# Two feature pairs instead of one go by halves of the tokens at the four norm joints of a three-block float32 kernel

## The chip, the cores and the metric

The kernel runs on one core of one Trainium2 chip. The metric is the device time of one execution in microseconds (us); a lower number is better. The engines are named as in the profile: PE is TensorE (its weight loads are PEld), DVE is VectorE, ACT is ScalarE, POOL is GpSimd and SP is SyncE, which here only issues transfers.

## The reference, cut to what matters

512 tokens of width 1024 go through a first block (mixer, then a mixture of 32 experts) and a second block of two layers:

```
x = first_block(x, ...)            # mixer, hier_moe (32 experts, 2 per token), rmsnorm(x, norm_final)
h = layer_norm(x, ln_in_g, ln_in_b)
for l in range(2):
    proj = h @ w_in[l]             # q, k, v, u
    a = diff_attention(q, k, v)    # 8 heads, softmax(s1) - lam * softmax(s2)
    f = fourier_mix(u, w_f[l], b_f[l])
    h = layer_norm(ALPHA * h + concat(a, f) @ w_o[l], ln1_g[l], ln1_b[l])
    g, up = split(h @ w_gu[l])     # 2 x 2816 columns
    h = layer_norm(ALPHA * h + (silu(g) * up) @ w_down[l], ln2_g[l], ln2_b[l])
return h
```

So a product follows each norm, and the product can only begin for those tokens whose norm is done.

## The kernel before, in words

**Products.** Every product of the second block is done in float32 accuracy by three matmuls (`mm3`, lines 507 to 509): weights and data are each split into a high part (fp32r) and the rest, and hi\*hi, hi\*lo and lo\*hi are added in PSUM. Weights come in chunks of 128 x 1024 values. SP loads a chunk into one of four raw cells (line 464); ACT copies it to its high part (`hi_to`, line 483); DVE subtracts to get the low part (`lo_to`, line 493). The parts lie in a ring of three slots; a chunk named in the list `apart` of `halves_places` takes a fourth slot, and then the ring goes on without it. A chunk may be converted when the product that used its slot last has counted `w_used`. A product of one feature pair (2 x 128 output features, 512 tokens) uses two chunks and 48 matmuls (`gemm_feat`).

**A norm joint.** There are four: the experts' sum with the final and the first norm (`*_final`), the norm behind `w_o` of each layer (`*_wo`), and the one behind `w_down` of layer 0 (`*_ffn`). The 512 tokens are four tiles. For each tile DVE adds the residual and takes statistics, POOL the root, ACT applies the norm (line 690; 2284 at the first joint), PE transposes it (line 599, `turn_pe`), ACT scales it (622) and writes the high part (626), and DVE writes the rest (630, 636). PE does the last chunks of the product ahead tile by tile between the transposes (`gemm_tail`), and then `feat_halves`: the first feature pair behind the norm, at first for tokens 0 to 255 (24 matmuls of 256 columns for one feature tile, the last tile's transposes, 24 more), and, when the last tile is done, for tokens 256 to 511 (48 more). The second feature pair follows as a whole by `gemm_feat` with 48 matmuls of 512 columns. In the feed-forward part the pairs are named gate and up, in the mixer Q and K.

**The barrier.** `meet` drains PE, ACT, DVE and POOL and lets each go on when all four have come. It stands at the end of `*_wo` and `*_ffn`, on PE behind `feat_halves`. The first joint has none.

**The mixer's start.** ACT issues five small loads (2601 to 2605), copies Q (2610), converts two chunks, splits the 128 x 128 constants and `w_f` (2613, 2615), loads the table of Exp and copies K (2620); DVE makes the low parts (2688 to 2715). PE forms an outer product of the two split constants (`w_mm`, 6 matmuls, waits for `spl` from DVE line 2708) and then the scores (2529), which wait for K's low part.

**Between experts and the second block.** The last experts' rows are scattered to DRAM (`s_y`) by POOL (2146). When the scatters have landed, four reloads are issued by SP (2259) and four by ACT (2274), two for each token tile. The vectors of the final and first norm are loaded by ACT (2102 to 2104), each broadcast to 128 partitions (512 KB).

**The down projection.** `gemm_tok` does 11 chunks for each half of the output. Its first matmul waits until POOL has written the low part of the last activation (2986).

## Time and profile before

| | |
|---|---|
| median of 3 runs | 2004.35 us (2002.73 to 2006.64) |
| the profiled execution: time, span | 2006.64 us, 2005.4 us |
| PE busy | 1838.4 us, 92% of the span |
| DVE, ACT, POOL busy | 958.5, 777.3, 394.9 us |
| mean granted clock of TensorE | 0.967 |

The time is that of a whole execution; the span is that between the first and the last instruction in its profile. PE is busy for 92% of the span, so the question at each place is for what PE waits there. Timeline rows give start, duration, engine, line, operation, output and input, a count, and in brackets the idle time before and what ended it. ACTq and SPq rows are transfers being issued.

### The profile page before, as it was taken

How to read it: one execution, taken by the hardware profiler on the slowest of the kernel's cores; microseconds unless marked ns; L12 is line 12 of the kernel's file. 1: busy time of each engine (PE TensorE's matmuls, PEld its weight loads, DVE VectorE, ACT ScalarE, POOL GpSimd, SP SyncE). 2: the span in 40 equal slices, each digit the busy share in tenths (PEclk: the TensorE clock that was granted, in tenths of full speed). 3: DMA queues.
4: the chain of work that ended last, by engine and by line, in shares of the span. 5: the costliest groups of instructions: out<-in, count | busy, mean ns of one | idle time of the engine just before them, and what ended most of it. 6: DMA issues, size and time to landing. Idle time of an engine off the chain costs nothing.

```text
span 2005.4 us, 26563 instructions
## 1 busy us (share of the span) xinstructions
PE 1838.4 (92%) x10396; PEld 1449.7 (72%) x10396; DVE 958.5 (48%) x1881; ACT 777.3 (39%) x1436; POOL 394.9 (20%) x438
## 2 busy tenths in 40 slices
PE   7999999996998754998999999999999999999997
PEld 6888777785544424776778888787876778888786
DVE  4458776663311015968454433234868454333234
ACT  3344476221433234665253233115566252332212
POOL 1019155102222111243011111000233012111001
PEclk9999999996999996998999999999998999999999
DMA  4244200576999983211323333232211233333231
GB/s 162 80 113 126 95 2 2 168 286 242 381 383 401 394 308 125 74 53 43 105 85 100 100 95 95 89 100 70 77 64 43 84 95 98 101 95 95 87 103 53
DMA packets 134884, 264.43 MB, mean 132 GB/s; under 512 B 11616, under 2 KB 92128, under 8 KB 122464
## 3 DMA queue, kind: packets, MB, share of 16 engines
q1 hardware_dynamic: 116320, 228.35, 33.1%
q10 hardware_dynamic: 13312, 25.90, 3.8%
q0 software_dynamic: 5120, 8.40, 1.3%
q8 instruction: 85, 1.39, 0.3%
q14 instruction: 47, 0.39, 0.1%
HBM read 254.22 MB, written 16.78 MB: 135 GB/s over the span
## 4 chain that ended last, share of the span: by engine, by line
PE 54%; DMA 9%; DVE 7%; ACT 3%; issue 2%; POOL 1%; PEld 1%; PEldq 0%; ACTq 0%; POOLq 0%; SPq 0%; DVEq 0%
PE b L507 15%; PE b L508 15%; PE b L509 15%; DMA m<-in_w_gate_up 6%; PE b L2023 3%; ACT m L622 2%; DVE m L2736 1%; DMA m<-in_w_down 1%; PE b L2561 1%; PE b L2048 1%; PE b L2543 1%; PE b L2529 1%; DMA s_h<-m 1%; ACT m L690 1%; DVE m L694 1%
## 5 line engine op out<-in xcount | busy, mean ns | idle before, releaser
L507 PE MATMUL b<-m,m 128*128 128x512 f32 (+3 forms) x2060 | 782.0, 380 | 28.4 <-DVE m L636 8.8
L508 PE MATMUL b<-m,m 128*128 128x512 f32 (+3 forms) x2060 | 772.6, 375 | 0.0
L509 PE MATMUL b<-m,m 128*128 128x512 f32 (+3 forms) x2060 | 772.5, 375 | 0.0
L493 DVE TENSOR_TENSOR m<-m,m 128x1024 fp32r<-128x1024 f32 (+1 forms) x212 | 278.2, 1319 | 497.5 <-ACT m L483 496.6
L507 PEld LDWEIGHTS b<-m,m 128*128 128x128 f32 x2060 | 392.6, 191 | 105.8 <-issue 22.1
L509 PEld LDWEIGHTS b<-m,m 128*128 128x128 f32 x2060 | 392.4, 190 | 67.5
L508 PEld LDWEIGHTS b<-m,m 128*128 128x128 f32 x2060 | 393.1, 191 | 64.1
L483 ACT ACTIVATE m<-m 128x1024 fp32r<-128x1024 f32 (+1 forms) x236 | 245.7, 1048 | 484.2 <-PE b L509 458.0
L2986 POOL TENSOR_TENSOR m<-m,m 128x512 fp32r<-128x512 f32 x44 | 71.1, 1636 | 422.1 <-ACT m L2932 422.1
L2023 PE MATMUL b<-m,m 128*64 128x256 f32 x1024 | 126.7, 390 | 27.5 <-DMA m<-in_w_gate_up 26.2
L2023 PEld LDWEIGHTS b<-m,m 128*64 128x64 f32 x1024 | 73.6, 139 | 78.9 <-issue 38.6
L2111 DVE SCALAR_TENSOR_TENSOR m<-m,m,b 64x256 f32<-64x256 f32 x32 | 15.4, 482 | 215.6 <-ACT m L2090 215.6
L2636 ACT ACTIVATE m<-m,m 128x512 f32<-128x512 f32 x128 | 91.0, 712 | 57.5 <-DVE m L2736 57.5
L2776 POOL TENSOR_TENSOR m<-m,m 128x1024 fp32r<-128x1024 f32 x24 | 61.8, 2573 | 175.5 <-PE b L2529 175.5
L2736 DVE CUSTOM_DVE_ANT_0 m<-b,m 128x512 f32<-128x512 f32 x128 | 80.6, 685 | 18.2 <-PE b L2529 18.2
L682 POOL TENSOR_TENSOR m<-m,m 128x1 f32<-128x1 f32 x20 | 13.7, 685 | 362.4 <-DVE m L678 330.6
L599 PE MATMUL b<-m,m 128*128 128x128 f32 x160 | 26.0, 315 | 52.5 <-ACT m L2284 33.0
L2048 PE MATMUL b<-m,m 128*64 128x512 f32 x256 | 62.0, 603 | 8.8 <-DMA m<-in_w_down 7.3
L2932 ACT ACTIVATE m<-m 128x512 fp32r<-128x512 f32 x44 | 27.8, 632 | 97.1 <-DVE m L2952 96.0
L599 PEld LDWEIGHTS b<-m,m 128*128 128x128 f32 x160 | 20.9, 161 | 59.2 <-ACT m L2284 34.7
L2099 ACT ACTIVATE m<-b 64x512 f32<-64x512 f32 x64 | 37.9, 592 | 51.0 <-PE b L2048 50.2
L2952 DVE TENSOR_TENSOR m<-b,m 128x512 f32<-128x512 f32 x44 | 30.2, 692 | 52.4 <-PE b L509 52.4
(339 smaller groups left out, 1896.2 us busy)
## 6 DMA issues: line engine op xcount, KB each, us to landing
m<-in_w_gate_up SPq DMA_DIRECT2D x64, 1024.0 KB
m<-in_w_gu SPq DMA_DIRECT2D x88, 512.0 KB, 3.5
m<-in_w_down SPq DMA_DIRECT2D x32, 1024.0 KB
m<-in_w_in SPq DMA_DIRECT2D x48, 512.0 KB, 3.8
m<-in_w_down SPq DMA_DIRECT2D x44, 512.0 KB, 3.7
m<-in_w_in SPq DMA_DIRECT2D x20, 448.0 KB, 3.6
m<-in_w_o SPq DMA_DIRECT2D x16, 512.0 KB, 3.8
s_gt<-m ACTq DMA_DIRECT2D x16, 256.0 KB, 2.1
```

Of the source, the lines that this page charges most:

```text
L483: e.activation(flat(whi[HX[i]], i), flat(raw[cell], i), ACT.Copy).then_inc(sem("w_hi"), 1)
L493: e.tensor_tensor(flat(wlo[HX[i]], i), flat(raw[RX[i][0]], i), fr(flat(whi[HX[i]], i)), ALU.subtract).then_inc(sem("w_lo"), 1)
L507: e.matmul(out, xh, yh, start=start, stop=False, skip_group_check=True)
L508: e.matmul(out, xh, yl, start=False, stop=False, skip_group_check=True)
L509: return e.matmul(out, xl, yh, start=False, stop=stop, skip_group_check=True)
L599: m = e.transpose(bank[b][:, k * P:k * P + P], src[:, (4 * g + k) * P:(4 * g + k + 1) * P], ident)
L2023: m = e.matmul(bank[i][CAP * h:CAP * h + CAP, 0:256], XT[i][:, k, :], w[:, kk, 256 * h:256 * h + 256], start=k == 0, stop=k == 7, skip_gro ...
L2048: m = e.matmul(bank[2 + i][CAP * h:CAP * h + CAP, :], AT[i][:, f, :], w[:, 0, 512 * h:512 * h + 512], start=f == 0, stop=f == 1, skip_grou ...
L2636: e.activation(x, x, ACT.Exp, bias=sm2[:, 0, 4 * s + j:4 * s + j + 1], scale=-1.0, accum_out=sm2[:, 2, 4 * s + j:4 * s + j + 1]).then_inc( ...
L2736: e.tensor_tensor_reduce(EE[s % 2][j], bank[j][:, :], m, 2.0 ** -(h + 1), 3e38, ALU.add, ALU.min, sm2[:, 0, w:w + 1]).then_inc(sem("m_m"), 1)
L2776: e.tensor_tensor(flat(wlo[HX[i]], i), flat(raw[RX[i][0]], i), fr(flat(whi[HX[i]], i)), ALU.subtract).then_inc(sem("w_lo"), 1)
L2986: e.tensor_tensor(FAl[:, k, :], UP[f], fr(FAh[:, k, :]), ALU.subtract).then_inc(sem("ff_l"), 1)
```

## The change

**The joints.** `feat_halves` now takes two feature pairs (four chunks, four banks). The first token half is done for both pairs, then the second half for both. The last tile's transposes come after the first feature tile at the first joint, and after the second one at the three others. The whole `gemm_feat` of the second pair (K, or the first up) is gone, so that `meet` now stands behind both pairs. The third and fourth chunk are converted ahead of ACT's and DVE's work on the third tile's gain (`t == 3`), no longer at the joint's end. `mix0` joins the chunks that have the fourth slot. Layer 1 swaps banks 0 to 3 with 4 to 7, in the mixer's outer product and scores too.

**The first joint.** The norm vectors are loaded by SP ahead of the first mixer chunks (`sync_gains`), and all eight reloads of `s_y` are issued by SP. The conversions of the first four mixer chunks stand at the start of `*_final`. ACT applies the norm of the last tile behind the gain of the third.

**The down projection.** Its first matmul waits for the bank and the first two activations only; after each chunk it waits for the next two (`after_down`).

```diff
-        HX, HB = halves_places(len(chunks), (CH["gu0"], CH["mix1"], CH["gu1"]), WHOLE)
+        HX, HB = halves_places(len(chunks), (CH["mix0"], CH["gu0"], CH["mix1"], CH["gu1"]), WHOLE)
...
-        def feat_halves(e, name, c0, xhi, xlo, bs, u, amid):
+        def feat_halves(e, names, c0, xhi, xlo, bs, u, amid, free):
-            w = [chunk(e, c0), chunk(e, c0 + 1)]
+            w = []
             for half in range(2):
                 c = slice(256 * half, 256 * half + 256)
                 e.wait_ge(*at("tr_lo", 8 * u + 4 * half + 4))
+                for q in range(2):
+                    if half == 0 and q == 1:
+                        free(e)
+                    for f, k in [(f, k) for f in range(2) for k in range(8)] if half == 0 else [(f, k) for k in range(8) for f in range(2)]:
+                        if half == 0 and f == 0 and k % 4 == 0:
+                            w.append(chunk(e, c0 + 2 * q + k // 4))
+                        hi, lo = w[2 * q + k // 4]
+                        sl = slice(f * P, f * P + P)
+                        m = mm3(e, bank[bs[2 * q + f]][:, c], hi[:, k % 4, sl], lo[:, k % 4, sl], xhi[:, k, c], xlo[:, k, c], k == 0, k == 7)
+                        if half == 1 and k == 7 and f == 0:
+                            m.then_inc(sem("mm_" + names[q]), 1)
+                        if half == 0 and k == 7:
+                            amid(2 * q + f)
+                    if half == 1:
+                        m.then_inc(sem("w_used"), 2)
...
         def vector_layer_norm(e, n, before, hi, lo, chunk_to):
                 ln_stats(e, n, t)
+                if t == 3:
+                    lo_to(e, chunk_to + 2)
...
         def scalar_layer_norm(e, n, hi, banks, chunk_to):
             for t in range(NT):
+                if t == 3:
+                    hi_to(e, chunk_to + 2)
...
-            return (lambda t: one(t - 1) if t > 0 else None), (lambda f: one(3) if f == 0 else None)
+            return (lambda t: one(t - 1) if t > 0 else None), (lambda n: one(3) if n == 1 else None)
...
+        def sync_gains(e):
+            last = max(i for i, cells, _ in LOADS if cells[0] in (TAIL + 4, GAINS))
+            e.wait_ge(*at("w_used", last + 2))
+            e.dma_start(gF, io["norm_final"].partition_broadcast(P)).then_inc(sem("gF"), 16)
+            e.dma_start(gL, io["ln_in_g_2"].partition_broadcast(P)).then_inc(sem("gL"), 16)
+            e.dma_start(bL, io["ln_in_b_2"].partition_broadcast(P)).then_inc(sem("gL"), 16)
...
             for t in range(NT):
+                e.dma_start(YA[2 * t], Y2[t * P:t * P + P, :]).then_inc(sem(f"ya{2 * t}"), 16)
                 e.dma_start(YA[2 * t + 1], Y2[S + t * P:S + t * P + P, :]).then_inc(sem(f"ya{2 * t + 1}"), 16)
...
         def scalar_final(e):
-            added_up(e)
-            for t in range(NT):
-                e.dma_start(YA[2 * t], Y2[t * P:t * P + P, :]).then_inc(sem(f"ya{2 * t}"), 16)
             e.dma_start(LNT, io["c_lnT"]).then_inc(sem("lnT"), 16)
+            hi_to(e, CH["mix0"] + 4)
...
         def tensor_mixer(e, l):
             c0 = CH[f"mix{l}"]
-            gemm_feat(e, f"k{l}", c0 + 2, NHhi, NHlo, 8, (6, 7), no_wait)
...
-            feat_halves(e, f"fg{l}", CH[f"gu{l}"], NHhi, NHlo, (0, 1), 3 + 2 * l, amid)
+            feat_halves(e, (f"fg{l}", f"up{l}"), CH[f"gu{l}"], NHhi, NHlo, swapped(l, (0, 1, 2, 3)), 3 + 2 * l, amid, lambda e: e.wait_ge(*at(f"res_wo{l}", 8)))
             meet(e)
...
             def free_down(e, j, t):
-                if t == 0:
-                    e.wait_ge(*at("ff_l", 22 * l + 22))
+                if t == 0 and j == 0:
+                    e.wait_ge(*at("ff_u", 22 * l + 20))
+                    e.wait_ge(*at("ff_l", 22 * l + 2))
+
+            def after_down(e, u):
+                if u < 10:
+                    e.wait_ge(*at("ff_l", 22 * l + 2 * u + 4))
...
         def sync_program(e):
             sync_norm1(e)
-            load_chunks(e, 0, CH["mix0"] + RAW)
+            load_chunks(e, 0, CH["mix0"])
+            sync_gains(e)
+            load_chunks(e, CH["mix0"], CH["mix0"] + RAW)
             sync_final(e)
```

**What the instructions look like in order.** On ACT, at layer 0's first norm joint, before: the gain of the last tile (m_56 and m_57, to m_214), the third and fourth chunk's high parts (into ring slots m_59, m_60 from raw cell m_54), and behind the barrier (`s_meet`) the feed-forward part.

```order
L622 ACTIVATE m_56<-b,m_206 128x128 [waits s_tr_lo,s_tr_pe]
L622 ACTIVATE m_56<-b,m_206 128x128 x3
L622 ACTIVATE m_57<-b,m_206 128x128 [waits s_tr_pe]
L622 ACTIVATE m_57<-b,m_206 128x128 x3
L626 ACTIVATE m_214<-m_56 128x4x128 [waits s_at_p]
L483 ACTIVATE m_59<-m_54 128x1024 [waits s_w_used,s_w_raw0]
L483 ACTIVATE m_60<-m_54 128x1024 [waits s_w_used,s_w_raw1]
L2913 DMA m_263<-in_ln_g 128x1024 [waits s_meet]
L2914 DMA m_264<-in_ln_b 128x1024
L2928 ACT_TABLE_LOAD
L2928 ACTIVATE m_259<-b 128x512 [waits s_mm]
```

The same place of the change, from the norm of the third tile to the gain of that tile, and then the rows about the barrier:

```order
L696 ACTIVATE m_127<-m_127,m_205 128x1024 [waits s_ln_nm]
L483 ACTIVATE m_58<-m_54 128x1024 [waits s_w_used,s_w_raw0]
L483 ACTIVATE m_59<-m_54 128x1024 [waits s_w_used,s_w_raw1]
L628 ACTIVATE m_56<-b,m_206 128x128 [waits s_tr_lo,s_tr_pe]
L628 ACTIVATE m_56<-b,m_206 128x128 x3
L628 ACTIVATE m_57<-b,m_206 128x128 [waits s_tr_pe]
L628 ACTIVATE m_57<-b,m_206 128x128 x3
L632 ACTIVATE m_214<-m_56 128x4x128 [waits s_at_p]
```

```order
L628 ACTIVATE m_57<-b,m_206 128x128 x3
L632 ACTIVATE m_214<-m_56 128x4x128 [waits s_at_p]
L2937 DMA m_263<-in_ln_g 128x1024 [waits s_meet]
L2938 DMA m_264<-in_ln_b 128x1024
L2952 ACT_TABLE_LOAD
L2952 ACTIVATE m_259<-b 128x512 [waits s_mm]
L2952 ACTIVATE m_260<-b 128x512 [waits s_w_used]
L483 ACTIVATE m_60<-m_55 128x1024 [waits s_w_used,s_w_raw2]
L483 ACTIVATE m_58<-m_55 128x1024 [waits s_w_used,s_w_raw3]
```

The two conversions (L483) moved from just ahead of the barrier to ahead of the third tile's gain; the rows behind the barrier are the same, but the fifth and sixth chunk (m_60 and m_58) are now the first that PE needs there, where before they were the third and fourth.

On SP, at the end of the experts' weights (m_136, m_137), before: the first mixer chunks (m_54, m_55) and the four reloads.

```order
L468 DMA m_136<-in_w_down 128x2048
L468 DMA m_137<-in_w_down 128x2048
L464 DMA m_54<-in_w_in 128x4x256 x2
L464 DMA m_55<-in_w_in 128x4x256 x2
L2259 DMA m_217<-s_y 128x1024
L2259 DMA m_219<-s_y 128x1024
L2259 DMA m_221<-s_y 128x1024
L2259 DMA m_223<-s_y 128x1024
```

And in the change:

```order
L468 DMA m_137<-in_w_down 128x2048
L2263 DMA m_201<-in_norm_final 128x1024
L2264 DMA m_202<-in_ln_in_g 128x1024
L2265 DMA m_203<-in_ln_in_b 128x1024
L464 DMA m_54<-in_w_in 128x4x256 x2
L464 DMA m_55<-in_w_in 128x4x256 x2
L2271 DMA m_216<-s_y 128x1024
L2272 DMA m_217<-s_y 128x1024
L2271 DMA m_218<-s_y 128x1024
L2272 DMA m_219<-s_y 128x1024
L2271 DMA m_220<-s_y 128x1024
L2272 DMA m_221<-s_y 128x1024
```

The three norm vectors (m_201 to m_203) now lie between the experts' weights and the mixer's chunks, and the reloads have become eight in a row, of which six are shown.

On ACT, at the start of the first mixer, before: the fourth chunk (m_59), five small loads, the copies of Q (to m_225), and the fifth and sixth chunk.

```order
L483 ACTIVATE m_59<-m_55 128x1024 [waits s_w_used,s_w_raw3]
L2601 DMA m_249<-in_c_c 128x256
L2602 DMA m_250<-in_w_f 128x4x128
L2603 DMA m_211<-in_lam_params 128x128
L2604 DMA m_212<-in_subln_g 128x1
L2605 DMA m_213<-in_b_f 128x4
L2610 ACTIVATE m_225<-b,m_209 128x512 [waits s_mm,s_bo]
L2610 ACTIVATE m_225<-b,m_209 128x512 [waits s_w_used]
L483 ACTIVATE m_60<-m_54 128x1024 [waits s_w_used,s_w_raw0]
L483 ACTIVATE m_58<-m_54 128x1024 [waits s_w_used,s_w_raw1]
L2613 ACTIVATE m_251<-m_249 128x256 [waits s_w1v]
```

And in the change:

```order
L2621 DMA m_249<-in_c_c 128x256
L2622 DMA m_250<-in_w_f 128x4x128
L2623 DMA m_211<-in_lam_params 128x128
L2624 DMA m_212<-in_subln_g 128x1
L2625 DMA m_213<-in_b_f 128x4
L2630 ACTIVATE m_225<-b,m_209 128x512 [waits s_mm,s_bo]
L2630 ACTIVATE m_225<-b,m_209 128x512 [waits s_w_used]
L483 ACTIVATE m_59<-m_54 128x1024 [waits s_w_used,s_w_raw0]
L483 ACTIVATE m_60<-m_54 128x1024 [waits s_w_used,s_w_raw1]
L2633 ACTIVATE m_251<-m_249 128x256 [waits s_w1v]
L2635 ACTIVATE m_253<-m_250 128x512 [waits s_g1]
```

The fourth chunk's conversion is gone from here. The sixth chunk now goes to m_60, the slot of the third chunk, which both versions free only when PE has used it; in the change that is at the end of K.

## Rows read from the trace of the kernel before

**Rows 1.** The page's first part, PE; then the waits of PE in total.

```profile
PE 1838.4 (92%) x10396; PEld 1449.7 (72%) x10396; DVE 958.5 (48%) x1881; ACT 777.3 (39%) x1436; POOL 394.9 (20%) x438
...
PE b L599 <- ACT m L2284: 33.0, 3, 25.9
...
PE b L507 <- DVE m L636: 8.8, 5, 2.8
...
PE b L507 <- POOL m L2986: 6.9, 2, 3.4
```

**Rows 2.** Timeline, experts' end to second block: start us, us, what, idle before it.

```profile
738.94 0.89 POOL L2146 DMA_INDIRECT s_y<-m,m  x1 [7.13 <-ACT m L2099]
...
742.48 0.89 POOL L2146 DMA_INDIRECT s_y<-m,m  x1 [2.65 <-ACT m L2099]
...
742.89 0.49 ACTq L2104 DMA_DIRECT2D m<-in_ln_in_b  x1
...
751.01 2.01 SPq L2259 DMA_DIRECT2D m<-s_y  x4
...
756.08 1.23 DVE L2307 TENSOR_TENSOR m<-m,m 128x1024 f32<-128x1024 f32 x1 [9.90 <-DMA m<-s_y]
...
782.20 0.55 PE L507 MATMUL b<-m,m 128*128 128x256 f32 x1 [2.85 <-DVE m L636]
```

**Rows 3.** DMA queues: windows 740:741, 747:748; then L2104's own landing.

```profile
q0 software_dynamic: 27, 0.11, 50.0%
...
q0 software_dynamic: 47, 0.10, 26.3%
...
DMA to landing us min/median/max: 8.3/8.3/8.3
```

**Rows 4.** Timeline of PE at layer 0's first norm joint.

```profile
1020.59 1.09 PE L599 MATMUL b<-m,m 128*128 128x128 f32 x8 [1.54 <-ACT m L690]
...
1026.02 0.38 PE L507 MATMUL b<-m,m 128*128 128x256 f32 x1 [1.48 <-DVE m L636]
...
1031.76 0.28 PE L509 MATMUL b<-m,m 128*128 128x256 f32 x1
1032.29 0.47 PE L507 MATMUL b<-m,m 128*128 128x512 f32 x1 [0.26 <-PEq L439]
...
1043.03 0.39 PE L509 MATMUL b<-m,m 128*128 128x512 f32 x1
```

**Rows 5.** Timelines of ACT and DVE behind that joint.

```profile
1032.12 0.34 ACTq L2913 DMA_DIRECT2D m<-in_ln_g  x1
...
1035.23 1.06 ACT L483 ACTIVATE m<-m 128x1024 fp32r<-128x1024 f32 x1
...
1036.39 1.23 DVE L493 TENSOR_TENSOR m<-m,m 128x1024 fp32r<-128x1024 f32 x1 [8.16 <-ACT m L483]
```

**Rows 6.** Timelines of ACT, DVE and PE at layer 1's mixer.

```profile
1406.59 0.34 ACTq L2601 DMA_DIRECT2D m<-in_c_c  x1
...
1412.58 1.06 ACT L483 ACTIVATE m<-m 128x1024 fp32r<-128x1024 f32 x1 [1.38 <-PE b L509]
...
1410.70 0.23 DVE L2688 TENSOR_TENSOR m<-m 128x64 f32<-128x64 f32 x1 [8.00 <-DMA m<-in_lam_params]
...
1415.15 0.69 DVE L2708 TENSOR_TENSOR m<-m,m 128x512 fp32r<-128x512 f32 x1
...
1419.33 0.51 PE L2529 MATMUL b<-m 32*128 32x512 f32 x4
```

**Rows 7.** Timeline of PE: layer 0's first scores.

```profile
810.88 0.51 PE L2529 MATMUL b<-m 32*128 32x512 f32 x4
```

**Rows 8.** PE at layer 0's down projection; then windows, PEclk behind POOL.

```profile
1264.44 0.77 PE L507 MATMUL b<-m,m 128*128 128x512 f32 x1 [3.43 <-POOL m L2986]
...
1264.40:1267.40 3.00, 2.96 (x7) 2.41 (x8) 0.98 (x1) 0.00 (x0) 0.00 (x0) 0.50 0.18 46
1267.40:1272.00 4.60, 4.60 (x21) 3.73 (x21) 0.00 (x0) 0.27 (x1) 0.00 (x0) 0.98 0.22 84
```

More of the change, by code:

```diff
@@ L581, in feat_halves @@
                 e.wait_ge(*at("tr_lo", 8 * u + 4 * half + 4))
-                for f, k in [(f, k) for f in range(2) for k in range(8)] if half == 0 else [(f, k) for k in range(8) for f in range(2)]:
-                    hi, lo = w[k // 4]
-                    sl = slice(f * P, f * P + P)
-                    m = mm3(e, bank[bs[f]][:, c], hi[:, k % 4, sl], lo[:, k % 4, sl], xhi[:, k, c], xlo[:, k, c], k == 0, k == 7)
-                    if half == 1 and k == 7 and f == 0:
-                        m.then_inc(sem("mm_" + name), 1)
-                    if half == 0 and k == 7:
-                        amid(f)
-            m.then_inc(sem("w_used"), 2)
+                for q in range(2):
[13 more added lines that the diff above has]
+                        m.then_inc(sem("w_used"), 2)
         def turn_pe(e, u, t, src, banks):
@@ L2342, in gpsimd_second, with lb, swapped @@
             c.inc(e.iota(TOE.bitcast(I32), pattern=[[-1, 896]], base=384, channel_multiplier=1))
+        def lb(l):
+            return bank[4 * l:] + bank[:4 * l]
+        def swapped(l, banks):
+            return tuple(b ^ (4 * l) for b in banks)
         NST = 16
@@ L2400, in block_job @@
             c0 = CH[f"mix{l}"] + BLK[f"{kind}{n - n % 2}"]
-            o = bank[jbank[j]]
+            o = lb(l)[jbank[j]]
             for tt in range(2 if kind == "V" else 1):
@@ L2420, in tensor_job @@
             kind, n = j[0], int(j[1])
-            o = bank[jbank[j]]
+            o = lb(l)[jbank[j]]
             bank_free(e, l, j, s)
@@ L2457, in scalar_job @@
             kind, n = j[0], int(j[1])
-            o = bank[jbank[j]]
+            o = lb(l)[jbank[j]]
             if kind not in "VQKUCD":
@@ L2481, in vector_job @@
             kind, n = j[0], int(j[1])
-            o = bank[jbank[j]]
+            o = lb(l)[jbank[j]]
             if kind in "UV":
@@ L2528, in tensor_scores @@
                     r = slice(32 * j, 32 * j + 32)
-                    m = e.matmul(bank[j][:, :], QT[a][r, p, qt * P:qt * P + P], KT[b][r, p, :], start=i == 0, stop=i == 2, skip_group_check=True)
+                    m = e.matmul(lb(l)[j][:, :], QT[a][r, p, qt * P:qt * P + P], KT[b][r, p, :], start=i == 0, stop=i == 2, skip_group_check=True)
                     if i == 2:
@@ L2548, in tensor_values @@
             p, half = m_ // 2, m_ % 2
-            o = bank[6][:, 256 * half:256 * half + 256]
+            o = lb(l)[6][:, 256 * half:256 * half + 256]
             e.wait_ge(*at("m_h", NST * l + 2 * m_ + 2))
@@ L2609, in scalar_mixer @@
                 q0_done(e, l, x)
-                e.activation(QT[0][:, x, :], bank[4 + x][:, :], ACT.Copy, scale=qsc[:, x:x + 1]).then_inc(sem("qk0_h"), 1)
+                e.activation(QT[0][:, x, :], lb(l)[4 + x][:, :], ACT.Copy, scale=qsc[:, x:x + 1]).then_inc(sem("qk0_h"), 1)
             hi_to(e, c0 + 3 + HL)
@@ L2658, in scalar_turn_p @@
             turned_free(e, l, k)
-            e.activation(*turned(k, 0), ACT.Copy).then_inc(sem("m_h"), 1)
+            e.activation(*turned(l, k, 0), ACT.Copy).then_inc(sem("m_h"), 1)
         def scalar_out(e, l, p):
@@ L2665, in scalar_out @@
                 e.wait_ge(*at("n_l", 4 * l + p - 1))
-            e.activation(OO[p % 2], bank[6][:, :], ACT.Copy).then_inc(sem("m_o"), 1)
+            e.activation(OO[p % 2], lb(l)[6][:, :], ACT.Copy).then_inc(sem("m_o"), 1)
             if p > 0:
                 job_done(e, l, f"B{p - 1}")
-            e.activation(SQ, bank[6][:, :], ACT.Square).then_inc(sem("m_o"), 1)
+            e.activation(SQ, lb(l)[6][:, :], ACT.Square).then_inc(sem("m_o"), 1)
         def scalar_normed(e, l, p):
```

82 lines of the change are left out of this document (38 added, 44 removed).

## Prediction

> **What bounds the kernel now.** I read the page first, then PE's waits in total, then the timeline at each place that the diff touches. PE is busy for 92% of the span, and each single reason for which it waits is small [rows 1]. The largest here is the first joint (33.0 us before the transposes). The change aims at it only at its edges. The others that it touches are the wait for the last tile's low part (8.8 us in 5 waits) and the start of the down projection (6.9 us in 2 waits). PE alone sets the pace behind the experts. So for each place I ask when PE's next matmul can start, and whether ACT and DVE have its operands ready by then.
>
> **The change part by part.**
>
> *1. Between experts and first joint.* POOL issues the last scatter of expert rows from 742.48 to 743.37, and ACT issues the norm vectors up to 743.4; SP gets the scatters' landing at 751.01, and the first pair of reloads is there at 756.08 [rows 2]. The last norm vector landed 8.3 us after its issue at 742.89, at 751.2 [rows 3]: at the same moment as the scatter. The scatter before was issued at 738.94 to 739.83 [rows 2] and its packets ran at 740 to 741, while those of the last one mostly wait until 747 [rows 3]. I read this as the scatter standing among 1.5 MB of norm vectors. In the change these are issued behind the last expert weights and ahead of the mixer's chunks. If the last scatter then needs what the one ahead of it did (through by about 742.5, so 2.7 us from the end of its issue), SP starts at 743.4 + 2.7 = 746.1 instead of 751.0: 4.9 us. The first pair's second reload is now issued 0.5 us behind the first on one queue (four issues take 2.01 us). Term: -4.5 us, with bounds of -5.4 (scatter through in 1.8 us) and 0 (it was late for another reason). The first four conversions on ACT and DVE are done by about 750 and lie in this wait.
>
> Here the Trainium skill ("DMA: Bandwidth & Descriptors", Queues, rings and completion order) speaks against this term: each DMA engine goes round between the queues that have work, a packet at a time. By that rule a scatter beside the vectors' queue would have been through soon, and their removal would bring little. The rows of queue 0 do not bear it out here (its packets come at 747), but they do not show the cause either.
>
> *2. Layer 0's norm joint, up to the barrier.* Before: the first feature tile ends at 1020.59 - 1.54 = 1019.05, PE waits 1.54 us for the last tile's norm, transposes, does the second feature tile, waits 1.48 us, and does the second half [rows 4]. From 1026.02 to 1031.76 lie 47 matmuls of 256 columns: 0.12 us each, 5.8 us for 48; from 1032.29 to 1043.03 lie 47 of 512: 0.228 us each, 10.97 us for 48. So a pair in halves costs 0.6 us more than whole. The pair "up" now ends at about 1043.3. After: from 1019.05 PE goes on with the second feature tile (2.9 us, to 1021.9), transposes (1.0 us), first half of the second pair (5.8), both second halves (11.6): the end is 1040.2. Does anything stop it? ACT has two conversions (1.06 us each [rows 5]) ahead of the third tile's gain, and waits for the product ahead to end, so the last tile's norm, which PE had at 1020.59, comes at about 1021.8: just in time. The last tile's low part follows its transposes by some 4.5 us (1026.02 - 1021.68 [rows 4]), and 5.8 us of second pair cover it. So both waits go, and PE stands at the barrier 3.1 us earlier than it finished the same work before.
>
> *3. Behind that barrier.* Before, PE had the whole pair "up" (11 us) there, and its chunks had been made ready ahead of `meet`. In that cover ACT issued two loads, loaded a table, did both Silu, and converted the next chunk from 1035.23; DVE's low part came from 1036.39 to 1037.62 [rows 5]. That is 5.5 us after ACT's first issue at 1032.12. Now PE's next product (gate of i = 1) needs this very chunk; nothing converts it earlier, since `chunk_to + 2` ends with the fourth. So PE stands still from 1040.2 for 0.25 us of barrier and 5.5 us of ACT and DVE, until about 1046.0: 2.7 us later than before (1043.3).
>
> *4. The clock.* After 3.43 us of idle time PE restarts at 1264.44 with a granted clock of 0.50, the 1.2 GHz level, until about 1267.4, and is at 0.98 on average behind it [rows 8]. Half of 3 us is a loss of 1.5 us. The waits of 1.5 us [rows 4] show nothing like it. Each new stall is longer than 3.4 us, so I add 1.5 us to each. Items 2 to 4 give +4.3 us for this joint and, with the same code in layer 1, +8.6 us for both.
>
> *5. Layer 1's mixer.* The joint is the same and lies 374.5 us later (ACT's first issue behind it is at 1406.59, not 1032.12 [rows 5, 6]), so its two pairs end at 1414.6. Only then ACT starts its five loads. In the trace ACT begins them at 1406.59, DVE is held until 1410.70 by the load of the lambdas, and is then busy nearly without a gap until `w_f` is split at 1415.15 + 0.69 = 1415.84 [rows 6]: 9.25 us. ACT's wait for PE in it (1.38 us) isn't on this chain. PE's outer product waits for it: 1414.6 + 0.25 + 9.25 = 1424.1. At half pace 6 matmuls take 2.6 us, and K's low part is there by then, so the scores start at 1426.7 to 1427.0 instead of 1419.33 [rows 6]. Term: +7.5 us (+6.3 if the clock stays up).
>
> *6. Layer 0's mixer.* No barrier here: the small loads and Q's copies stay hidden. The first half starts at 782.20 [rows 2] (all shifted by item 1). Counted back from the scores at 810.88 [rows 7]: outer product 1.6, whole K 11.0, second half 5.8, a wait like that of item 2 (1.6) leave the second feature tile's end at 790.9; with the second pair's first half (5.8) and both second halves (11.6) behind it, less the 0.3 between them that goes, the end is 808.0. The sixth chunk's slot becomes free only then, and on ACT its conversion stands ahead of the constants, `w_f`, and K. From such a conversion at 1412.58 to the split `w_f` at 1415.84 layer 1 took 3.3 us [rows 6], so the outer product starts at 808.0 + 0.25 + 3.3 = 811.5, and with a halved clock the scores start at 814.2 instead of 810.88. Term: +3.4 us (+2.5 at full clock).
>
> *7. Down projections.* The wait of 3.43 us [rows 8] goes in both layers: the first two activations and the bank are long ready, and the last activation is needed only after 10 chunks of 5.5 us. With the 1.5 us at half clock behind it: -5.0 us each, -10.0 us.
>
> Sum: -4.5 + 8.6 + 7.5 + 3.4 - 10.0 = +5.0 us, on the profiled execution's 2006.64 us. That one lies 2.3 us above the median, so I predict 2004.35 + 5.0, about 2009.5 us. The banks and the swap cost nothing: the products' count and sizes stay, and no bank is waited for by this reading.
>
> **The rivals.**
>
> *A, faster:* the stalls behind the barriers and in front of the outer products don't come, because the next chunk's conversion turns out to lie ahead of the barrier. Then each joint gives its 2.7 us (1043.3 - 1040.2, less 0.4 of barrier), the first mixer about 1 us, and the sum is -4.5 - 8.1 - 1 - 10.0 = -24 us: 1980 us. Against it: the order on ACT has that conversion behind the rows with `s_meet`. It decides as soon as the restart takes less than 2.7 us instead of 5.5. Chance 0.07.
>
> *B, the scatter isn't held by the norm vectors:* the DMA engines serve both in turn, and the scatter is late through something of its own. Then SP starts at 751.0 as before and item 1 is 0: 2009.5 + 4.5 = 2014 us. For it: its first packets do run beside the vectors; against it: the scatter ahead of it was quick [rows 3]. Chance 0.2. It is the case that the Trainium skill's rule in item 1 stands for.
>
> *C, the clock doesn't fall* in the new stalls, or only for a part: 4 x 1.5 less, 2003.5 us, no change to be measured. For it: only one restart is read here. Against it: it is the only kind of restart from more than 3 us that this place shows [rows 8]. Chance 0.13.
>
> *D, the down projection's wait comes back* as one for a weight chunk (the third chunk's slot is freed only when the last "up" ends): 2009.5 + 10 = 2019.5 us. Against it: two chunks are ready, 11 us of work, and ACT and DVE need 2.3 us for a chunk. Chance 0.05.
>
> **How the numbers follow.** My forecast (all seven items) has 0.55. The range must reach to B and to C: 2002 to 2016 us. Two executions of this kernel differ by up to 3.9 us, so 0.2% (4 us) is about what can be told from no change. Slower (over 2008.4): most of the forecast, B and D; same: C and the forecast's lower edge; faster: A and little else. That gives 0.60 slower, 0.30 same, 0.10 faster.
>
> **What would show it.** In the profile after: no wait of PE for DVE's last low part (line 636's counterpart) behind the second layer norms; new waits of PE for the low part of a weight chunk (493) of 5 to 6 us behind both `*_wo`, about 9 us for the split of `w_f` in layer 1 and 3 to 4 us in layer 0; granted clock 0.50 after each; no wait for the activation's low part at the down projections; SP's reloads about 3 us after the last scatter's issue, not 8. I am wrong if PE passes the barriers without a stall, or if the scatter still lands 7.6 us after its issue.

## The result, and the profile after

The change takes 2009.66 us (median of 12 runs, 2006.6 to 2014.37), the kernel before beside it 2004.47 us (12 runs, 2000.53 to 2008.14). The ratio is 1.0022 (95% interval 1.0014 to 1.0031), so the change is slower by 5.2 us, and the forecast said 5.0. The profiled execution took 2009.88 us with a span of 2008.3 us and a mean granted clock of 0.961, where before had 0.967.

The page's first part of the change, PE; then PE's waits in total. They answer to [rows 1].

```profile
PE 1840.8 (92%) x10588; PEld 1463.3 (73%) x10588; DVE 956.6 (48%) x1881; ACT 776.5 (39%) x1436; POOL 395.0 (20%) x438
...
PE b L605 <- ACT m L2294: 30.5, 3, 23.4
...
PE b L507 <- DVE m L493: 16.3, 5, 5.7
PE b L507 <- DVE m L2728: 12.7, 2, 9.3
...
PE b L507 <- DVE m L642: 2.7, 1, 2.7
```

The reader is to see that PE's busy share has not moved while its list of waits has. The wait for POOL's last activation at the down projection (6.9 us) is gone, and of the 8.8 us for the last tile's low part 2.7 are left, all at the first joint. Two waits have grown in their place: one for the low part of a weight chunk (L493) and one for the low part of `w_f` (L2728), which is not among the waits of before. For the weight chunks before had this row:

```profile
PE b L507 <- DVE m L493: 4.9, 3, 2.0
```

The timeline of the change between experts and first joint, as in [rows 2]:

```profile
740.48 0.89 POOL L2151 DMA_INDIRECT s_y<-m,m  x1 [2.65 <-ACT m L2109]
745.34 0.34 ACTq L2285 DMA_DIRECT2D m<-in_c_lnT  x1
745.73 3.90 ACT L483 ACTIVATE m<-m 128x1024 fp32r<-128x1024 f32 x4 [6.02 <-issue]
746.58 0.34 SPq L2271 DMA_DIRECT2D m<-s_y  x1
746.81 4.63 DVE L493 TENSOR_TENSOR m<-m,m 128x1024 fp32r<-128x1024 f32 x4 [13.30 <-ACT m L483]
...
751.55 1.23 DVE L2323 TENSOR_TENSOR m<-m,m 128x1024 f32<-128x1024 f32 x1
```

SP starts the reloads 5.2 us after the end of the last scatter's issue (741.37), where before it was 7.6 us. ACT passes the branch at the experts' end in 6 us without work and converts the first four chunks only behind it. DVE's four low parts end at 751.4, just when the first sum begins.

The timeline of PE at layer 0's norm joint, as in [rows 4], then those of ACT and DVE behind the barrier, as in [rows 5]:

```profile
1018.77 1.04 PE L605 MATMUL b<-m,m 128*128 128x128 f32 x8
...
1036.56 0.28 PE L507 MATMUL b<-m,m 128*128 128x256 f32 x1
...
1042.80 0.77 PE L507 MATMUL b<-m,m 128*128 128x512 f32 x1 [5.73 <-DVE m L493]
```

```profile
1037.16 0.33 ACTq L2937 DMA_DIRECT2D m<-in_ln_g  x1
...
1040.27 2.00 ACT L483 ACTIVATE m<-m 128x1024 fp32r<-128x1024 f32 x2
...
1041.43 2.36 DVE L493 TENSOR_TENSOR m<-m,m 128x1024 fp32r<-128x1024 f32 x2 [17.33 <-ACT m L483]
```

The last tile's transposes stand without idle time, and PE then runs at 0.12 us for each matmul of 256 columns up to the barrier. There it stops for 5.73 us, until ACT and DVE have loaded a table, done the two Silu and converted the fifth chunk.

The timelines of PE at the two mixers' starts, as in [rows 6, 7]:

```profile
803.88 0.28 PE L509 MATMUL b<-m,m 128*128 128x256 f32 x1
807.56 0.80 PE L507 MATMUL b<-m,m 128*128 128x512 f32 x1 [3.40 <-DVE m L2728]
...
810.41 0.80 PE L2550 MATMUL b<-m 32*128 32x512 f32 x4
...
1410.21 0.28 PE L509 MATMUL b<-m,m 128*128 128x256 f32 x1
1419.74 0.77 PE L507 MATMUL b<-m,m 128*128 128x512 f32 x1 [9.25 <-DVE m L2728]
...
1422.57 0.80 PE L2550 MATMUL b<-m 32*128 32x512 f32 x4
```

Busy time in windows of the change, the granted clock behind POOL's column: behind layer 0's barrier, over the start of layer 0's down projection, and at layer 0's mixer, as in [rows 8]:

```profile
1042.80:1045.90 3.10, 3.10 (x7) 2.48 (x8) 3.10 (x4) 1.47 (x3) 0.70 (x1) 0.50 0.61 184
...
1249.00:1280.00 31.00, 31.00 (x139) 25.66 (x138) 8.64 (x8) 8.60 (x10) 2.54 (x2) 1.00 0.32 102
...
807.50:810.40 2.90, 2.84 (x6) 1.82 (x6) 2.13 (x6) 1.72 (x4) 0.00 (x0) 0.50 0.58 181
810.40:813.80 3.40, 3.40 (x21) 2.64 (x21) 2.44 (x7) 1.45 (x4) 0.00 (x0) 0.50 0.00 0
```

The clock falls to its 1.2 GHz level behind each new stall. The down projection begins without a stall and at full clock.

**Where the 5 us are.** I cut both profiles at the same seven starts on PE and at the end of the last scatter's issue (743.37 before, 741.37 after). That leaves out everything ahead, where the code is the same and single profiles differ by some us. Each column is one execution.

| stretch (us) | before | after | difference | predicted |
|---|---|---|---|---|
| last scatter to first halves | 38.83 | 36.20 | -2.6 | -4.5 (item 1) |
| to layer 0's first scores | 28.68 | 32.84 | +4.2 | +3.4 (item 6) |
| to layer 0's last scores | 129.06 | 127.31 | -1.8 | 0 |
| to the first transposes behind `w_o` | 63.39 | 62.61 | -0.8 | 0 |
| to those behind `w_down` (joint, down) | 374.45 | 373.41 | -1.0 | -0.7 (items 2 to 4, 7) |
| to layer 1's first scores | 41.55 | 48.83 | +7.3 | +7.5 (item 5) |
| to layer 1's last scores | 127.99 | 128.96 | +1.0 | 0 |
| to the transposes behind layer 1's `w_o` | 63.16 | 62.88 | -0.3 | 0 |
| to PE's end (joint, down) | 382.77 | 381.68 | -1.1 | -0.7 (items 2 to 4, 7) |
| sum | 1249.88 | 1254.72 | +4.8 | +5.0 |

### The profile page after: what moved, and what is told of

Its sections match the earlier page's. It is cut to its first block, busy times and chain, and to the rows that moved or that the text cites. A ratio compares the mean times of both kernels' runs of the same rounds, so it can differ in the third digit from the quotient of the medians.

```text
span 2008.3 us, 26967 instructions
## 1 busy us (share of the span) xinstructions
PE 1840.8 (92%) x10588; PEld 1463.3 (73%) x10588; DVE 956.6 (48%) x1881; ACT 776.5 (39%) x1436; POOL 395.0 (20%) x438
## 4 chain that ended last, share of the span: by engine, by line
PE 56%; DMA 9%; DVE 4%; PEld 3%; ACT 2%; issue 1%; POOL 1%; PEldq 0%; ACTq 0%; POOLq 0%; SPq 0%; DVEq 0%
PE b L507 16%; PE b L508 15%; PE b L509 15%; DMA m<-in_w_gate_up 6%; PE b L2033 3%; PE b L2582 2%; DMA m<-in_w_down 2%; PE b L2564 1%; PE b L2550 1%; PE b L2058 1%; PEld b L507 1%; PEld b L509 1%; PEld b L508 1%; ACT m L628 1%; DMA s_h<-m 1%
## 5 line engine op out<-in xcount | busy, mean ns | idle before, releaser
L507 PE MATMUL b<-m,m 128*128 128x512 f32 (+3 forms) x2124 | 793.6, 374 | 36.5 <-DVE m L493 16.3
L508 PE MATMUL b<-m,m 128*128 128x512 f32 (+3 forms) x2124 | 784.5, 369 | 0.0
L509 PE MATMUL b<-m,m 128*128 128x512 f32 (+3 forms) x2124 | 784.3, 369 | 0.0
L493 DVE TENSOR_TENSOR m<-m,m 128x1024 fp32r<-128x1024 f32 (+1 forms) x212 | 278.2, 1320 | 502.0 <-ACT m L483 500.9
L507 PEld LDWEIGHTS b<-m,m 128*128 128x128 f32 x2124 | 406.0, 191 | 109.3 <-issue 33.4
L509 PEld LDWEIGHTS b<-m,m 128*128 128x128 f32 x2124 | 406.0, 191 | 63.9
L508 PEld LDWEIGHTS b<-m,m 128*128 128x128 f32 x2124 | 406.6, 191 | 61.6
L483 ACT ACTIVATE m<-m 128x1024 fp32r<-128x1024 f32 (+1 forms) x236 | 245.3, 1048 | 471.5 <-PE b L509 439.1
L605 PEld LDWEIGHTS b<-m,m 128*128 128x128 f32 x160 | 21.2, 162 | 51.5 <-ACT m L2294 32.2
L2952 ACT ACTIVATE m<-b 128x512 f32<-128x512 f32 x44 | 26.1, 598 | 74.4 <-PE b L509 72.8
```

The source lines that it names most:

```text
L483: e.activation(flat(whi[HX[i]], i), flat(raw[cell], i), ACT.Copy).then_inc(sem("w_hi"), 1)
L493: e.tensor_tensor(flat(wlo[HX[i]], i), flat(raw[RX[i][0]], i), fr(flat(whi[HX[i]], i)), ALU.subtract).then_inc(sem("w_lo"), 1)
L507: e.matmul(out, xh, yh, start=start, stop=False, skip_group_check=True)
L508: e.matmul(out, xh, yl, start=False, stop=False, skip_group_check=True)
L509: return e.matmul(out, xl, yh, start=False, stop=stop, skip_group_check=True)
L605: m = e.transpose(bank[b][:, k * P:k * P + P], src[:, (4 * g + k) * P:(4 * g + k + 1) * P], ident)
```

## The experiments

The first four ran on one chip (before there: 2005.19 us), the next four on a second (2004.9), the last four on a third (2005.01). The change ran beside a kernel before of 2004.47 us, so a difference to the change can be off by 0.5 to 0.7 us for that alone; the ratios are to the kernel before on the same chip.

**undo_down**: the down projection waits for the last activation again.

```diff
-                if t == 0 and j == 0:
-                    e.wait_ge(*at("ff_u", 22 * l + 20))
-                    e.wait_ge(*at("ff_l", 22 * l + 2))
+                if t == 0:
+                    e.wait_ge(*at("ff_l", 22 * l + 22))
...
-swapped(l, B03)], free_down, after_down, tail=3
+swapped(l, B03)], free_down, tail=3
```

> The change with the old wait at the down projection (its first matmul waits for the last activation's low part) and nothing else undone. My sum: the wait of 3.4 us and 1.5 us at half clock come back in both layers, about 10 us over the change: 2019 to 2020 us, with an idle row of 3.4 us and a granted clock of 0.50 behind it at both places. Rival (the pause only lets ACT and DVE get ahead with weight chunks, and without it PE pays the same a few chunks later): no difference from the change, about 2009.5 us.

Measured: 2022.51 us (2020.8 to 2024.29), ratio to before 1.0092 (1.0075 to 1.0109), so 12.9 us more than the change. The timeline of PE and two windows behind it:

```profile
1263.58 0.77 PE L507 MATMUL b<-m,m 128*128 128x512 f32 x1 [3.42 <-POOL m L3007]
...
1263.60:1266.60 3.00, 3.00 (x7) 2.42 (x8) 0.92 (x1) 0.00 (x0) 0.00 (x0) 0.50 0.24 53
1266.60:1269.20 2.60, 2.60 (x7) 1.99 (x7) 0.00 (x0) 0.00 (x0) 0.00 (x0) 0.50 0.36 140
```

The stall is that of before to 0.01 us, but PE now stays at 1.2 GHz for 5.7 us (1263.58 to 1269.26), where it was about 3 us in [rows 8]. With the same at layer 1 (6.1 us) the two stalls cost 3.4 + 2.8 and 3.4 + 3.0, 12.7 us; the two stretches with the down projection are 6.5 and 6.7 us longer than in the change, 13.2 us. That is more than the 10 us expected, and the longer half clock isn't a mark of this edit. before_apart (below) is the kernel before at this place, with the same stalls (3.43 and 3.42 us), and had both lengths in one execution:

```profile
1256.90:1263.00 6.10, 6.10 (x15) 4.74 (x16) 0.89 (x1) 0.00 (x0) 0.00 (x0) 0.50 0.28 86
...
1864.30:1867.10 2.80, 2.80 (x7) 2.22 (x8) 0.93 (x1) 0.00 (x0) 0.00 (x0) 0.50 0.22 32
```

**undo_vectors**: ACT loads the norm vectors at the experts' end again.

```diff
             e.wait_ge(*at("w_used", CH["mix0"]))
+            e.dma_start(gF, io["norm_final"].partition_broadcast(P)).then_inc(sem("gF"), 16)
+            e.dma_start(gL, io["ln_in_g_2"].partition_broadcast(P)).then_inc(sem("gL"), 16)
+            e.dma_start(bL, io["ln_in_b_2"].partition_broadcast(P)).then_inc(sem("gL"), 16)
...
-            sync_gains(e)
```

> The change with the three norm vectors loaded by ACT behind the last expert again; all eight reloads of the expert rows stay on SP. My term: the last scatter is held by the vectors, SP's first reload comes 7 to 8 us after the end of the scatter's issue instead of about 3, and the time is 4.9 us over the change: 2014 to 2015 us. Rival B (the scatter is late by itself): reload and time as in the change, 2009 to 2010 us.

Measured: 2013.67 us (2009.68 to 2014.76), ratio 1.004 (1.0025 to 1.0055), 4.0 more than the change. The timeline of this kernel at the experts' end:

```profile
740.97 0.89 POOL L2154 DMA_INDIRECT s_y<-m,m  x1 [2.66 <-ACT m L2109]
...
748.32 0.34 SPq L2274 DMA_DIRECT2D m<-s_y  x1
...
753.82 1.22 DVE L2326 TENSOR_TENSOR m<-m,m 128x1024 f32<-128x1024 f32 x1
```

The scatter is in 6.5 us after the end of its issue (741.86), not 5.2, and not the 7 to 8 us expected. The first halves start 37.98 us after it, 1.8 us later than in the change. The vectors do hold the scatter, here by 1.3 us. ACT issues them from 739.00 here, 2.0 us ahead of the scatter; before it was 0.4 us ahead (742.04 against 742.48), so 1.3 us need not be what they cost there. The other 2.2 us of the difference lie elsewhere in the run (1.5 of them in layer 0's mixer).

**fifth_early**: the change, with the fifth chunk converted ahead of the barrier.

```diff
         def vector_layer_norm(e, n, before, hi, lo, chunk_to):
...
             gained_lo(e, n, 3, hi, lo)
+            lo_to(e, chunk_to + 3)
...
         def scalar_layer_norm(e, n, hi, banks, chunk_to):
...
             gained_act(e, n, 3, hi, banks)
+            hi_to(e, chunk_to + 3)
```

> The change with the fifth chunk converted by ACT and DVE ahead of the barrier, behind their work on the last tile. If PE's stall behind both first norms of the layers is the wait for this chunk (5.5 us and 1.5 us of halved clock), each shrinks to the 0.3 us of the barrier: 13 to 14 us, and in layer 1's mixer 1.2 us of DVE's chain go too; 1994 to 1996 us. If the clock costs nothing: 1998. Rival: the sixth chunk, converted behind the table load and Silu, is then late by nearly as much, and only 2 to 5 us are won: 2005 to 2008 us.

Measured: 1995.8 us (1992.79 to 2000.1), ratio 0.9958 (0.9941 to 0.9976), 13.9 less than the change. The timeline of PE behind layer 0's joint:

```profile
1038.67 0.47 PE L507 MATMUL b<-m,m 128*128 128x512 f32 x1 [0.26 <-PEq L439]
...
1050.85 0.50 PE L507 MATMUL b<-m,m 128*128 128x512 f32 x1 [1.03 <-DVE m L493]
```

Two added calls take the 5.73 us and the half clock behind them away, at both layers (the two stretches with a joint are 5.6 and 5.7 us shorter than in the change; of the rest, 2.1 us are in layer 1's mixer). PE then waits 1.03 us for the next chunk, and that stall leaves the clock up. This is the largest single fault of the change.

**one_pair**: the change with one pair by halves as before, the second pair whole behind the barrier, and the third and fourth chunk converted at the joint's end; vectors, reloads, banks and down projection as in the change.

```diff
-            feat_halves(e, (f"fg{l}", f"up{l}"), CH[f"gu{l}"], NHhi, NHlo, swapped(l, (0, 1, 2, 3)), 3 + 2 * l, amid, lambda e: e.wait_ge(*at(f"res_wo{l}", 8)))
+            feat_halves(e, (f"fg{l}",), CH[f"gu{l}"], NHhi, NHlo, swapped(l, (0, 1)), 3 + 2 * l, amid, no_wait)
...
-                if i == 0:
-                    continue
-                gemm_feat(e, f"gate{l}", c0, NHhi, NHlo, 8, (o, o + 1), free_gate)
+                if i > 0:
+                    gemm_feat(e, f"gate{l}", c0, NHhi, NHlo, 8, (o, o + 1), free_gate)
...
+            gemm_feat(e, f"k{l}", c0 + 2, NHhi, NHlo, 8, swapped(l, (6, 7)), no_wait)
```

> The change with one feature pair by halves at each joint and the second pair whole behind the barrier, as before; the third and fourth chunk are again converted at the joint's end. Vectors, reloads, banks and down projections stay as changed. If the doubled halves are what costs, the time is that of before less 4.5 us (vectors) and 10 us (down): 1989 to 1991 us. Rival (the joints gain by the second pair, and the loss lies in the banks, the eight reloads on one queue or the first four conversions): above 2009 us.

Measured: 1989.04 us (1988.23 to 1991.15), ratio 0.9921 (0.9904 to 0.9938). The side edits alone are worth 16.2 us (0.8%). The second pair by halves turns them into a loss, at a cost of about 21 us (20.6 between the two medians, 21.3 with each taken against the kernel before on its own chip). one_pair has the joints of before and the new down projections, so it gives item 7 by itself: its two stretches with a down projection take 369.31 and 377.45 us, 5.1 and 5.3 us less than before.

**consts_early**: the change, with the mixer's small loads, the splits of constants and `w_f`, and the exponential ahead of Q's copies (layer 0) and ahead of the barrier of layer 0's feed-forward part (layer 1), and with K's parts ahead of the sixth chunk. `scalar_constants` holds the loads, the two splits and the exponential of ACT; DVE has its counterpart.

```diff
         def scalar_mixer(e, l):
...
+            if l == 0:
+                scalar_constants(e, l)
...
-            hi_to(e, c0 + 3 + HL)
+            hi_to(e, c0 + 2 + HL)
...
                 e.activation(KT[0][:, x - 2, :], lb(l)[4 + x][:, :], ACT.Copy).then_inc(sem("qk0_h"), 1)
+            hi_to(e, c0 + 3 + HL)
...
                 scalar_layer_norm(e, 2, NHhi, B47, CH["mix1"] + 2)
+                e.wait_ge(*at("w_used", CH["dn0"] + 22))
+                scalar_constants(e, 1)
```

> The change, with the five small loads of the mixer, the high and low parts of the constants and of w_f, and the exponential of the lambdas moved ahead of Q's copies in layer 0, and to the end of the feed-forward part of layer 0 (ahead of its barrier) for layer 1; K's high and low part stand ahead of the sixth chunk's conversion. My theory (the outer product waited only because ACT and DVE make these parts behind the barrier or behind the sixth chunk): both waits of PE for w_f's low part go (3.4 us in layer 0, 9.25 us in layer 1), and part of the half clock behind them, so 11 to 14 us less than the change, 1996 to 1999 us; in exchange PE may wait a little for K's low part or for the fifth chunk. Rival (the loads or the table of the exponential only move their time ahead of the barrier, where the norm joint is just in time): a new wait of PE for the last tile's norm in layer 0's second joint of 3 us or more, and 2002 us or more.

Measured: 2010.97 us (2006.65 to 2012.32), ratio 1.0029 (1.002 to 1.0038): no gain over the change, and neither theory. Both waits for `w_f` fell as I thought (28.41 us instead of 32.84 to layer 0's scores, 41.53 instead of 48.83 to layer 1's: 11.7 us). But the two mixers behind them grew from 127.31 to 134.44 us and from 128.96 to 133.16 us, which is 11.3 us. The timeline of POOL and DVE in layer 0's mixer:

```profile
815.33 1.22 DVE L700 TENSOR_TENSOR m<-m,m 128x1024 f32<-128x1024 f32 x1
816.01 2.79 POOL L2806 TENSOR_TENSOR m<-m,m 128x1024 fp32r<-128x1024 f32 x1 [35.58 <-PE b L2550]
816.59 3.30 DVE L649 TENSOR_TENSOR m<-m,m 128x1024 f32<-128x1024 f32 x1
824.97 2.38 POOL L2806 TENSOR_TENSOR m<-m,m 128x1024 fp32r<-128x1024 f32 x1 [6.17 <-ACT m L483]
825.27 3.16 DVE L700 TENSOR_TENSOR m<-m,m 128x1024 f32<-128x1024 f32 x1
```

The same operation of DVE takes 1.22 us alone and 3.2 to 3.3 us when POOL's is under way: it ends when POOL's (816.01 + 2.79 = 818.80) and then its own 1.1 us are over. The two do not share, one of them waits. The Trainium skill ("SBUF — State Buffer", SBUF: two separate sides) says so: a VectorE instruction with two SBUF inputs and a GpSimd instruction that reads SBUF exclude each other for the whole instruction. These rows agree. There are three such operations of DVE in each mixer here, and none in the change. My reading is that the scores, now 4.4 us earlier in layer 0, moved DVE's additions onto POOL's conversions. The change isn't free of collisions, though: there it is POOL that comes second (2.85 us instead of 2.34 at 834.93, and twice in layer 1), and DVE's operations keep their 1.22 us.

**both_early**: fifth_early and consts_early together.

> The edits of fifth_early and consts_early together. If the stalls behind the barriers and before the outer products are all that makes the change slower than before, it has none left and ends near 2009.7 - 13.9 (measured for the fifth chunk) - 11 to 14, that is 1982 to 1985 us, faster than one_pair (1989.0). If the two edits share a gain (the same late ACT and DVE work shows up once at either place) it ends above 1988.

Measured: 1991.62 us (1987.48 to 1993.37), ratio 0.9928 (0.9915 to 0.9941). It lies above 1988, but not because the two share a gain: the joints keep theirs (367.78 and 375.95 us, as in fifth_early), and so do the mixers' starts (27.83 and 42.63 us). Layer 0's mixer has three long operations of DVE again and takes 133.88 us. Layer 1's has none of DVE but three of POOL (up to 3.32 us) and takes 126.93.

**conv_early** and **all_early**: the first four mixer chunks are converted ahead of the branch at the experts' end, in the change and in both_early.

```diff
             e.wait_ge(*at("w_used", CH["mix0"]))
+            hi_to(e, CH["mix0"] + 4)
 
         def vector_experts(e):
...
+            lo_to(e, CH["mix0"] + 4)
 
         def gpsimd_experts(e):
...
         def scalar_final(e):
...
-            hi_to(e, CH["mix0"] + 4)
```

> The change, with the conversions of the first mixer chunks on ACT and DVE moved back ahead of the branch at the experts' end, where three of four stood in the kernel before. In the change DVE's fourth low part ends at 751.44 and the first sum of the reloads starts at 751.55 without idle time. Theory 1 (these conversions hide the reloads' landing, so that the missing 2 us of item 1 lie in them): the first sum starts 1 us or more sooner after the last scatter, with 2008 to 2008.7 us in all. Theory 2 (the reloads land about 5 us after SP's first issue in both kernels, so the conversions only fill the wait): DVE now idles until the reloads land, the first sum stays 9.7 to 10.4 us behind the last scatter's issue, and the time stays at 2009.7 within 1 us.

> both_early and conv_early together. Theory 1 of conv_early: 1 us or more less than both_early; theory 2: equal to both_early within 1 us.

Measured: conv_early 2014.99 us (2013.72 to 2016.87), 5.3 more than the change; all_early 1997.93 us (1994.78 to 2000.32), 6.3 more than both_early. Both theories fell, since neither had a loss in it. What SP waits for in conv_early at the experts' end:

```profile
SPq L2165 <- DMA s_y<-m,m: 8.5, 1, 8.5
...
SPq L2273 <- ACTq L2286: 3.5, 1, 3.5
```

The scatter is in at 746.8, 4.6 us after the end of its issue. Then SP waits 3.5 us more for ACT, which reports the branch as passed (`over`) only behind its conversions. In the kernel before three conversions stood there too, and SP's last 0.4 us were a wait for ACT as well. With the branch late, moving the vectors gains nothing: from the scatter to the halves it takes 39.19 us here, 38.83 before.

**before_apart, consts_apart, both_apart, one_apart**: one wait more on POOL in steps 1 to 4 of each mixer, in the kernel before, consts_early, both_early and one_pair.

```diff
         def gpsimd_mixer(e, l):
...
                     e.wait_ge(*at("m_s", 4 * (NST * l + s) + 1))
+                    if s <= 4:
+                        e.wait_ge(*at("ln_ov", 8 * l + s))
```

> The kernel before, with one edit: in the mixer GpSimd makes the low part of a weight chunk in steps 1 to 4 only when VectorE has finished the two additions of the same token tile (one wait more, 8 waits in all). In the kernel before one of these 128x1024 operations of VectorE took 3.32 us instead of 1.22 at 834.08, beside GpSimd's own. If the two engines cannot do such operations at once, this one is 1.22 again and layer 0's mixer is about 2 us shorter: 2002.5 to 2004 us, within what a measurement can tell. Rival (it was something else): one operation of over 3 us stays, and the time is the same.

> consts_early with the same wait on GpSimd. In consts_early six operations of VectorE took 3.1 to 3.3 us (three in each mixer) beside GpSimd, and the two mixers from the first to the last scores took 134.4 and 133.2 us, against 127.3 and 129.0 in the change. Theory (the collisions eat what the early constants gain): none is over 1.3 us, both mixers take 126.5 to 129 us, and the time is 1998 to 2001 us, 10 to 12 less than consts_early (2010.97). Rival (the early constants delay something else in the mixers, and the long operations are only seen beside it): the mixers stay above 131 us and the time above 2005 us.

> both_early with the same wait on GpSimd. In both_early only layer 0's mixer had three such operations and took 133.9 us (layer 1: 126.9). Theory: 1991.62 less about 6.5, 1984 to 1986.5 us. Rival: above 1989 us.

> one_pair with the same wait on GpSimd. It had one operation of 3.39 us in each mixer, worth about 1.7 us each: 1989.04 less 3.4, 1985 to 1987.5 us. With both_apart it tells whether the second pair by halves is worth anything once nothing waits behind it: two pairs save the waits of 1.5 us for the last tile at two joints and cost 0.6 us each at the halves' smaller matmuls, so I expect the two within 2 us of each other.

| kernel | without the wait (us) | with it (us) | ratio to before, with it | mixers without / with (us) |
|---|---|---|---|---|
| before | 2005.01 | 2001.48 | 0.9986 (0.9977 to 0.9995) | 129.06, 127.99 / 126.44, 126.67 |
| consts_early | 2010.97 | 1999.33 | 0.9963 (0.9949 to 0.9976) | 134.44, 133.16 / 127.85, 129.45 |
| both_early | 1991.62 | 1986.69 | 0.9912 (0.9899 to 0.9926) | 133.88, 126.93 / 127.83, 126.90 |
| one_pair | 1989.04 | 1987.67 | 0.9914 (0.99 to 0.9927) | 129.00, 128.47 / 126.75, 126.63 |

The timeline of consts_apart at the place shown above:

```profile
814.15 1.22 DVE L700 TENSOR_TENSOR m<-m,m 128x1024 f32<-128x1024 f32 x1
815.40 1.22 DVE L649 TENSOR_TENSOR m<-m,m 128x1024 f32<-128x1024 f32 x1
816.80 2.41 POOL L2808 TENSOR_TENSOR m<-m,m 128x1024 fp32r<-128x1024 f32 x1 [37.55 <-DVE m L649]
```

No operation of DVE of this size is over 1.3 us in the mixers of the four kernels, and none of POOL over 2.5 us. consts_apart is 11.6 us faster than consts_early, 10.3 of them in the two mixers, so the collisions were what had eaten the gain and not a companion. Those that make DVE wait are the dear ones: both_early's layer 1 mixer, where only POOL waits, takes 126.93 us, and 126.90 without any collision. before_apart is the kernel before with one wait more, and it is faster by 3.5 us, more than the 1 to 2.5 expected. one_apart and both_apart come out within 1 us of each other, and both beat the two kernels compared here. Both lie 0.2 us above their expected ranges; one_apart's gain of 1.4 us lies below the 3.4 expected, with ranges that overlap, so one collision in each mixer can't be told from the noise there.

## Why the prediction was right, and where it was off

The main line held: the side edits gain, and the second pair by halves loses more behind the barriers than it gains ahead of them.

*Item 1* is the term that was mis-sized: -2.6 us measured, -4.5 predicted. The step that failed is the 2.7 us that "the one ahead of it did" was said to need: that was read from when its packets ran, not from when it landed. Where the profile has the landing, it is later. These are the last two scatters of before_apart, whose code is that of before there, and then those of one_pair, whose vectors are moved as in the change; the time counts from the start of the issue, which takes 0.89 us:

```profile
DMA to landing us min/median/max: 5.1/5.1/5.1
DMA to landing us min/median/max: 8.6/8.6/8.6
...
DMA to landing us min/median/max: 6.1/6.1/6.1
DMA to landing us min/median/max: 5.8/5.8/5.8
```

So even the scatter ahead of the vectors took 4.2 us from the end of its issue, not 2.7, and with the vectors gone the last one is no slower than the one ahead of it (4.9 and 5.2 us). SP's first reload came 5.0 to 5.8 us behind the scatter in the change and the eight variants that have its vectors and its conversions. With the vectors beside it the last scatter took 6.5 us (undo_vectors), 7.2 us (before) and 7.7 us (before_apart): they cost it some 1.3 to 2.5 us. The Trainium skill's rule (rival B), that the two would be served in turn, had it right that moving the vectors would bring less than the 4.9 us of item 1, but it was not nothing.

The item also looked at one cause where there were two. In the kernel before, scatter and ACT's `over` came within 0.4 us of each other. The gain needed both the vectors moved (undo_vectors: 1.8 us lost) and the conversions taken from ahead of the branch (conv_early: 3.0 us lost). I had counted the second as free.

*Items 2 and 3*: no wait for the last tile at either joint, and 5.73 us of stall against 5.5 + 0.25. fifth_early shows that its cause is the fifth chunk's conversion. *Item 4*: the half clock behind the two barriers lasted 3.1 us in layer 0 and 3.4 us in layer 1, a loss of 1.6 and 1.7 us against 1.5. Rival C is out. That it came so close is luck in part: behind the same stall of 5.73 us it lasted 5.9 us in conv_early (1047.50 to 1053.4).

*Item 5*: 9.25 us of stall as said, +7.3 against +7.5. *Item 6*: 3.40 us of stall against 3.3 + 0.25, +4.2 against +3.4 because the first halves' way to the stall took 0.8 us longer. 0.7 us of that are the clock again, which stayed at 0.50 for 5.4 us from the halves' start (777.57), against 4.1 us before (782.20). Behind both outer products the half clock went on into the scores (until 813.8 and 1424.8), which items 5 and 6 left out: by my estimate from these times 1.7 and 1.1 us, if PE sets the pace there.

*Item 7*: -5.0 each fits both stretches, and one_pair measured 5.1 and 5.3 by themselves. Rival D did not come.

What no item had: the two stretches of layer 0's mixer and its `w_o` were 2.5 us shorter in spite of the half clock, and layer 1's mixer was 1.0 us longer. The kernel before had one long operation of DVE in layer 0's mixer and three of POOL, the change only one of POOL. Two of them from the timeline of before:

```profile
826.55 3.17 POOL L2776 TENSOR_TENSOR m<-m,m 128x1024 fp32r<-128x1024 f32 x1 [4.70 <-PE b L2529]
...
834.08 3.32 DVE L643 TENSOR_TENSOR m<-m,m 128x1024 f32<-128x1024 f32 x1
```

before_apart, which removes them all, shortens the same two stretches by 3.5 us (2.6 and 0.8). But the collision isn't shown as the cause of the 2.5 us. undo_down and undo_vectors have the change's mixer and no long operation of DVE, and took 129.3 and 128.8 us for it, as much as before (129.06), where the change took 127.31. Over all kernels without a long operation of DVE in layer 0's mixer the two stretches lie between 189.0 and 192.7 us (before: 192.45). One collision can't be told from that spread; three can, at 197.3 to 197.8 us. So a part of the forecast's accuracy is chance: item 1 fell short by 1.9 us, item 6 and layer 1's mixer cost 1.8 us more, and what paid for most of it, 2.5 us in layer 0's mixer and `w_o`, stood in no item and its cause is open.

## What to carry to other kernels

When work is pulled ahead of a barrier, look at what it had covered behind it: the next operands have to be pulled ahead too, or the wait moves and brings the slow clock with it. When operations shift by some us, compare the durations of the same operation on DVE and POOL before and after; a 1.2 us operation of DVE that takes 3.3 us was a collision here, and one wait was cheaper than it. A term that "the landing of X" decides should be read from landings, not from packets, and should name everything that its waiter waits for, since the second in line takes over at once. Before a stretch of one profile is explained, compare it with the same stretch in the other kernels that share its code.
